# Attention of a hybrid encoder block: one pipeline of 64 units instead of four of 16, gates from high and low parts, loads moved between queues

## The reference, cut to what matters

```python
h = rmsnorm(x) * (1 + scale1) + shift1
proj = h @ w_in      # DeltaNet q,k,v,z | small | q_b,k_b,v_b (8 heads of 64) | gate_a, gate_b (1024 each)
o_a = deltanet(...)  # 4 heads of 128, both directions, chunks of 64 tokens
o_b = neighbourhood_attention(q_b, k_b, v_b, rpb)  # grid of 8 rows x 64 columns, window 8 x 16, bias per head
x = x + gate1 * ((sigmoid(gate_a) * (o_a @ w_oa) + sigmoid(gate_b) * (o_b @ w_ob)) @ w_out)
x = x + gate2 * expert_choice_moe(rmsnorm(x) * (1 + scale2) + shift2)   # 16 experts
y = rmsnorm(x) * final_g
```

## Time and profile before

| what | value |
|---|---|
| median of three runs | 2696.39 us |
| the profiled execution: its own time, its span | 2698.65 us, 2696.9 us |
| busy of the span: TensorE, VectorE, ScalarE, GpSimd | 92%, 55%, 43%, 16% |
| mean granted clock of TensorE | 0.955 |
| project, deltanet, attention, merge begin at | 86, 431, 819, 1203 us |
| route begins, experts run until | 1350, 2670 us |

### The profile page before, as it was taken

How to read it: one execution, slowest core, us unless ns; L and a number is a source line. 1 busy time by engine, 2 the same in 40 slices (tenths; PEclk the granted TensorE clock), 3 DMA queues, 4 the chain that set the end, 5 groups by cost and what they waited for, 6 DMA issues and landing times. The chain is left out here.

```text
span 2696.9 us, 39301 instructions
## 1 busy us (share of the span) xinstructions
PE 2470.2 (92%) x14796; PEld 1778.2 (66%) x14796; DVE 1488.6 (55%) x1764; ACT 1157.7 (43%) x1302; POOL 432.7 (16%) x382
## 2 busy tenths in 40 slices
PE   7799998898996999987999399999999999999994
PEld 2677886777773444443344388888888888888883
DVE  2645212555541222221211588888888888888884
ACT  2422111222212323321111377667766676777763
POOL 2101202333311000001123101111111111111101
PEclk9899998999987999998999599999999999999997
DMA  6354311000005212127221599999999999999994
GB/s 220 126 180 154 116 63 64 18 23 28 22 2 126 70 47 70 43 80 255 70 109 62 187 357 375 375 372 380 374 376 374 370 376 376 374 373 373 372 376 150
DMA packets 269040, 556.74 MB, mean 206 GB/s; under 512 B 13192, under 2 KB 66541, under 8 KB 266893
## 3 DMA queue, kind: packets, MB, share of 16 engines
q1 hardware_dynamic: 255485, 517.51, 53.4%
q0 software_dynamic: 4608, 16.78, 2.4%
q10 hardware_dynamic: 8848, 21.04, 2.2%
HBM read 511.21 MB, written 44.07 MB: 206 GB/s over the span
## 5 line engine op out<-in xcount | busy, mean ns | idle before, releaser
L2273 PE MATMUL ps<-whigh,xeT 128*128 128x512 f32 x2048 | 668.7, 400 | 9.1 <-DVE xeT L2418 9.1
L2426 DVE TENSOR_TENSOR wlow<-hT,whigh 128x2048 fp32r<-128x2048 f32 x192 | 431.9, 2284 | 84.3 <-ACT whigh L2369 84.3
L2273 PEld LDWEIGHTS ps<-whigh,xeT 128*128 128x128 f32 x2048 | 386.9, 189 | 100.1 <-issue 9.5
L2273 PE MATMUL ps<-wlow,xeT 128*128 128x512 f32 x1024 | 406.5, 397 | 0.0
L2369 ACT ACTIVATE whigh<-hT 128x2048 fp32r<-128x2048 f32 x192 | 358.5, 1910 | 17.8 <-PE ps L2273 17.8
L2273 PE MATMUL ps<-whigh,hidT 128*128 128x512 f32 x1024 | 334.6, 398 | 1.5 <-DVE hidT L2453 1.5
L2426 DVE TENSOR_TENSOR wlow<-oaT,whigh 128x2048 fp32r<-128x2048 f32 x96 | 216.7, 2285 | 50.2 <-ACT whigh L2369 50.2
L1601 PE MATMUL ps<-hT,wg 128*128 128x512 f32 x512 | 241.4, 616 | 0.0
L2426 DVE TENSOR_TENSOR wlow<-obT,whigh 128x2048 fp32r<-128x2048 f32 x96 | 217.8, 2284 | 29.6 <-ACT whigh L2369 29.6
L2273 PEld LDWEIGHTS ps<-whigh,hidT 128*128 128x128 f32 x1024 | 192.8, 188 | 47.9 <-issue 1.7
L2273 PEld LDWEIGHTS ps<-wlow,xeT 128*128 128x128 f32 x1024 | 193.5, 189 | 43.2
(11 more groups left out here) (279 smaller groups left out, 3262.7 us busy)
## 6 DMA issues: line engine op xcount, KB each, us to landing
hT<-in_w_down SPq DMA_DIRECT2D x66, 1024.0 KB, 8.5
obT<-in_w_up SPq DMA_DIRECT2D x64, 1024.0 KB, 8.6
hT<-in_w_up SPq DMA_DIRECT2D x64, 1024.0 KB, 6.2
hT<-in_w_gate SPq DMA_DIRECT2D x62, 1024.0 KB, 9.0
oaT<-in_w_down SPq DMA_DIRECT2D x62, 1024.0 KB, 6.8
oaT<-in_w_gate SPq DMA_DIRECT2D x34, 1024.0 KB, 8.8
obT<-in_w_gate SPq DMA_DIRECT2D x32, 1024.0 KB, 5.7
oaT<-in_w_ada SPq DMA_DIRECT2D x16, 1024.0 KB, 7.1
```

The costliest lines, as they stand in the source:

```text
L2273: mm = pe.matmul(out, lhs[x], rhs[y], start=start and i == 0, stop=stop and i == 2)
L2426: dve.tensor_tensor(wlow[slot][:, :], raw[(FIRST + x) % RAW_SLOTS], whigh[slot][:, :].bitcast(F32), ALU.subtract).then_inc(low_done, 1)
```

## The change

The four turns of the attention loop become one unrolled pipeline of 64 units: the outputs of pair h are turned in slots 16h+12 and 16h+20 and the v of the next pair in slots 16h+14 and 16h+22, between other work; SLOTS is 70. q and k have two buffers each, v one, and are loaded in the final order, since project's `take` now writes q, k, v in column order and scales q. The gates are computed from `hh`, `hl` (kept from project) and split gate weights, three fp32r matmuls a step, 12 a slot. `rel` is loaded, and `outside` built, at the start and at the end of deltanet's lists; several buffers move into `m["hT"]` and `m["obT"]` to make room. In merge the nine loads go from ScalarE's queue to SP's, one or more behind each turn's loads, and the weights go ahead of the gates.

```diff
@@ phase_project, take
-                        func = ACT.Silu if tile < A_TILES else ACT.Copy
-                        act.activation(out[u % 4][:, :], ps[:, u % 4, :], func).then_inc(taken, 1)
+                        if tile < A_TILES:
+                            act.activation(out[u % 4][:, :], ps[:, u % 4, :], ACT.Silu).then_inc(taken, 1)
+                        else:
+                            act.activation(out[u % 4][:, :].rearrange("p (c r) -> p r c", r=ROWS),
+                                           ps[:, u % 4, :].rearrange("p (r c) -> p r c", r=ROWS), ACT.Copy,
+                                           scale=(-DH ** -0.5 if tile < A_TILES + PAIRS else 1.0)).then_inc(taken, 1)
@@ phase_deltanet, SP (first in its list) and GpSimd (last in its list)
+                for c in range(16):
+                    src = bass.AP(a["rpb"].tensor, RPB_FRONT - 15 * c - 8, [[HB * RPB_LEN, ROWS], [RPB_LEN, HB], [1, RPB_RUN]])
+                    sp.dma_start(rel[8 * c:8 * c + 8, :, :], src).then_inc(rel_in, 16)
...
                 make_ro(NU - 1)
+                pool.memset(outside[:, :], 0.0).then_inc(outside_done, 1)
+                for step, (lo, hi, x0, x1, base, slope, cm) in enumerate((
...
+                    pool.wait_ge(outside_done, step + 1)
...
+                    pool.affine_select(out=part, in_=part, compare_op=ALU.is_ge, fill=BIG, base=base + slope * x0,
+                                       pattern=[[slope, x1 - x0], [0, 8]], channel_multiplier=cm).then_inc(outside_done, 1)
@@ phase_attention, SP
+                load_pair(0)
+                load_gate(0)
+                load_v(0)
+                load_gate(1)
+                load_pair(1)
+                for tile in range(2, GTILES):
+                    load_gate(tile)
...
@@ phase_attention, TensorE
+                def gates(count):
+                    for _ in range(count):
+                        u, r = divmod(next(products), TERMS)      # TERMS = 3 * KD
+                        k, term = divmod(r, 3)
+                        tile, g = divmod(u, GROUPS)
+                        if r == 0:
+                            pe.wait_ge(glo_done, tile + 1)
+                            if u >= 1:
+                                pe.wait_ge(gate_sb, u)
+                        w = (ghi, ghi, glo)[term][tile % 2][:, k, :]
+                        x = (hh, hl, hh)[term][:, k, g * SEQ:(g + 1) * SEQ]
+                        mm = pe.matmul(ps[:, 1, :], w, x, start=(r == 0), stop=(r == TERMS - 1))
...
+                for w in range(SLOTS):
+                    if w < NW:
+                        scores(w)
+                    if w in V_AT:
+                        turn_v(*V_AT[w])
+                    if 2 <= w < NW + 2:
+                        turn(w - 2)
+                    if w in OUT_AT:
+                        turn_out(*OUT_AT[w])
+                    if 3 <= w < NW + 3:
+                        values(w - 3)
+                    if w < NW:
+                        gates(PER_SLOT)
@@ phase_attention, ScalarE: the high part, in slots with w % 4 == 1; VectorE: the low part, w % 4 == 2
+                def split(tile):
+                    act.wait_ge(wg_in[tile % 2], 16 * (tile // 2 + 1))
+                    if tile >= 2:
+                        act.wait_ge(gate_ps, GROUPS * (tile - 1))
+                    act.activation(ghi[tile % 2][:, :, :], wg[tile % 2][:, :, :], ACT.Copy).then_inc(ghi_done, 1)
@@ phase_merge, SP
-                with sp.Fori(0, KD // 2) as jj:
+                for jj in range(KD // 2):
                     for i in range(2):
                         sp.wait_ge(wide_done, jj * (2 * JOBS) + 4 * (i + 1))
-                        sp.dma_start(graw[i]...)   # gates first, then weights
+                        sp.dma_start(wj[i][:, 0:HA, :], ...)
+                        sp.dma_start(wj[i][:, HA:KD, :], ...)
+                        sp.dma_start(graw[i][:, :, :], ...)
+                    if jj == 0:
+                        sp.dma_start(late["wout"]...)
+                    if jj == 1:
+                        sp.dma_start(late["wr"]...), (late["mul2row"]...), (norm2...), (late["gate1"]...)
+                    if jj == 2:
+                        sp.dma_start(m["hT"]..., a["x"]...)
+                    if jj == 3:
+                        sp.dma_start(late["shift2"]...), (m["gate2"]...) twice
@@ phase_merge, ScalarE
-                act.wait_ge(graw_in[0], 16)
-                ... the same nine loads, ahead of the loop of sigmoids
```

More of the change, by code:

```diff
@@ L831, in phase_deltanet @@
         ro = sb("ro", [P, TPG])
-        on = sb("on", [P, TPG, P])
+        on = first["on"]
+        rel, outside = first["rel"], first["outside"]
         tokk_ps = sem("tokk_ps")
@@ L1443, in phase_attention @@
     KIND_AT = [0, 256, 640]
-    BIAS_W = 896
+    hh, hl = m["hh"], m["hl"]
+    rel, outside = first["rel"], first["outside"]
     with ExitStack() as ctx:
@@ L1561, in _ @@
[L1561 to L1570 removed]
+                for h in range(PAIRS):
@@ new lines, in turn_v @@
+                def turn_v(h, g):
+                    if g == 0:
+                        pe.wait_ge(v_in, 16 * (h + 1))
+                    if h >= 1:
+                        pe.wait_ge(ob_done, GROUPS * (h - 1) + g + 1)
+                    if h >= 1 or g >= 1:
+                        pe.wait_ge(vtok_sb, GROUPS * h + g)
+                    for t in range(TPG):
+                        mm = pe.transpose(ps[:, 0, t * P:(t + 1) * P], vT[:, g, t * P:(t + 1) * P], ident)
+                    mm.then_inc(vt_ps, 1)
@@ new lines, in turn_out, with scores @@
+                def turn_out(h, g):
+                    pe.wait_ge(otok_done, PER_PAIR * h + (g + 1) * 2 * TPG)
+                    pe.wait_ge(vtok_sb, min(GROUPS * (h + 1) + g, GROUPS * PAIRS))
+                    if h + g:
+                        pe.wait_ge(ob_done, GROUPS * h + g)
+                    for t in range(TPG):
+                        mm = pe.transpose(ps[:, 0, t * P:(t + 1) * P], otok[:, g, t, :], ident)
+                    mm.then_inc(obT_ps, 1)
+                def scores(w):
+                    h, g, hp, t = unit(w)
+                    k0, k1 = KEY_TILES[t]
+                    if w % PER_PAIR == 0:
+                        pe.wait_ge(qk_in[h % 2], 32 * (h // 2 + 1))
+                    if w >= 2:
+                        pe.wait_ge(sc_done, w - 1)
+                    rows = slice(hp * DH, (hp + 1) * DH)
+                    pe.matmul(ps[:, 2 + w % 2, 0:width(t)], qT[h % 2][rows, g, t * P:(t + 1) * P],
+                              kT[h % 2][rows, g, k0 * P:k1 * P], start=True, stop=True).then_inc(s_ps, 1)
@@ new lines, in _ @@
+                for w in range(SLOTS):
[11 more added lines that the diff above has]
+                        gates(PER_SLOT)
+                assert not list(products)
```

420 lines of the change are left out of this document (191 added, 229 removed).

## The result

The changed kernel takes 2612.76 us (median of 4 runs, 2599.64 to 2631.30) against 2697.52 for the kernel before on the same chip (4 runs, 2696.34 to 2698.88). The ratio is 0.969, 95% interval 0.9664 to 0.9716, so it is 84.8 us faster. The forecast was 2602. The four times lie 32 us apart, where those of before lie 2.5 us apart here (20 us on another chip, 2684.16 to 2703.87), and the profiled execution is the slowest of them: 2631.30 us, span 2629.6.

What follows compares the result with a forecast made beforehand. TensorE's list was taken to bound attention (busy 348.07 of 366 us). Slots and boundaries 69.9, opening 5.85, merge 1.5 and 17.7, less 0.5 in project, make 94.5 us less, so 2602; 8-in-10 range 2589 to 2623.

Steps and rivals of the forecast that it cites:

- part 3: Attention's opening: reordering copies go, splits come; first gate product at about 832.0, not 837.85, gain 5.85; rel's loads cost nothing.
- Part 1: Attention slots: twelve fp32r matmuls replace four fp32 products; a slot takes 4.44 us, not 5.15, saving 45.4 over 64 slots.
- the prediction's own sign: Attention: gate starts wider than 0.227, or a phase longer than 315 us, would show the first part wrong.
- Part 2: Attention's three pair boundaries: one pipeline leaves only a plain slot at each; net gain 25.4 us, bounds 20 and 29.
- Part 4: Merge: first job 1.5 us earlier; without stalls the first three turns take 89.5 us, not 107.17, gain 17.7.
- rival 1: Merge: one ordered queue makes blocks wait behind w_out or x, so only its start gains; 2620 us, chance 0.06.
- Part 5: Project's end: the last take writes with a stride, 1.12 us against 0.60, adding 0.5 us.
- Rivals 2, 3 and 4: Attention: another engine's chain sets slots (2647 or 2618, 0.06); fp32r matmuls cost 0.395 (2731, 0.02); waits tie units (2625, 0.02).

Runs made afterwards that it cites:

- rel spread: Changed kernel with rel's 16 loads issued three at a time behind the loads of units 2 to 7: 2608.9 us, ratio 0.9678.
- rel wide: Changed kernel with the 16 loads carrying the same bytes over 128 partitions, from w_in: 2606.56 us, ratio 0.9675.
- shift of 32 bytes: Rel's loads spread as above, plus a 32-byte buffer ahead of the split gate weights and another ahead of the experts' split weights: 2606.71 us.
- better order: Rel's loads spread, outside built before the last ro, first gate weights loaded ahead of the first pair: 2605.87 us, ratio 0.967; 2609.16 on another chip.
- the two moves: On top of rel's spread loads: outside built before the last ro, and first gate weights loaded ahead of the first pair; 2605.87 us with both.
- the paced kernel: Changed kernel with each of rel's 16 loads issued only when the one before has landed: 2637.96 us.

## Why the prediction was right, and where it was not

**Total.** 2602 forecast, 2612.76 measured; on a second chip the same kernel took 2628.55. Without the stalls it is 2606 to 2609 in four kernels (rel spread, rel wide, shift of 32 bytes, better order). The mechanism of every gain was right; one step had a cost that I put at nothing, and one price was too low.

**The step that failed, part 3:** "`rel` is no wait any more: its 16 issues stand first in deltanet's SP list, ahead of the load of unit 2, which is wanted some 50 us later; cost nothing." The load of unit 2 was in fact in time (it landed at 489.56 us and TensorE never waited for it). What stood in no list of mine was the transfer of TensorE's own instructions. It cost 20.3 us in the profiled execution, 16.6 of them in the two long stalls; by the medians it is 3.9 us (2612.76 against 2608.9, two chips) to 22.7 (2628.55 against 2605.87 on one chip, the two moves in it). That the loads cause it is shown by taking them away, doubling them, adding them to the kernel before, and changing only their shape. That it goes by way of TensorE's instruction packets rests on their times, on the count of instructions between two of them, on stalls inside groups, and on the paced kernel; no row names the engine that a packet is for, and what delays the packets is not shown.

The Trainium skill, Runtime: NRT & Kernel Launch, section "Instruction fetch mechanics", says that each sequencer fetches its instructions over a DMA queue of its own in blocks of 16 KiB (256 instructions), "mostly hidden". The trace agrees with the block: packets of 16 KB, 4 to 5 us apart where TensorE issues 64-column products, with a median of 247 of its instructions between two. The Trainium skill, DMA: Bandwidth & Descriptors, section on why a DMA increments its semaphore by 16 and not by 1, says that a transfer gets the largest number of engines up to 16 that divides the slowest dimension of both its sides; 8 partitions would get 8. The trace agrees: a DMA share of 0.53 from 466.00 to 475.30 us, when rel's packets are nearly alone, at 63 GB/s; over 128 partitions the share was 0.81 at 290 GB/s (the loads of two units in it). Put together the two would have pointed at the rival that my list lacked.

**Part 1, slots.** 45.4 forecast, 40.3 measured. The count of products and the rest of a slot (1.72 us) were right; the term that was mis-sized is the spacing, 0.2267 taken from project where attention has 0.2340: 768 x 0.0073 = 5.6 us. By the prediction's own sign (gate starts wider than 0.227) this price was wrong. My bound said that no row had one cheaper than 0.227; I had not looked for dearer ones, though the experts' rows of the kernel before show them (0.234).

**Part 2, boundaries.** 25.4 forecast, 23.6 measured, within 20 to 29. **Part 3's opening** itself: 5.85 against 6.3. First gates came 9.46 us behind the first issue (9.9 forecast), and the 2.8 us of selects are there (2.76). **Part 4:** 19.2 forecast, 18.9 in the changed kernel and 20.3 alone. Turns of 29.20 us; the queue's margins held, so rival 1 (one ordered queue) did not come. The first job was 1.2 us slower than the row of before (9.99 against 8.79); its mean granted clock was 0.69 against 0.79. **Part 5:** 0.5 forecast; the last take went from 0.60 to 1.08 us, and deltanet's start is 1.6 later, 1.1 of which no step of mine explains (the other profiles with this project phase have it 0.3 to 1.8 later). Rivals 2, 3 and 4 are out: from 900 to 1100 us TensorE was busy in all of the 200 us, a product cost 0.234 and not its length of 0.395, and between the first gate product and the end of attention TensorE's longest idle time was 0.5 us.

**The range** holds the measured total, but for the wrong reason: its upper end was set by rivals that did not happen, and a loss that was not listed moved the total towards it. That is luck: the same kernel's 2628.55 on the second chip lies outside 2589 to 2623.

## What to carry to other kernels

A load that "nothing waits for" can still hold up the transfers that bring instructions. Before placing a batch of loads of few partitions, ask how long it will drain (bytes over the rate of a like row, here 2.9 MB at 63 GB/s, 46 us) and which engine runs dense, short instructions meanwhile; spread the batch behind later units, or give it 128 partitions. And take a product's price from all rows of its kind, the dear ones too: two streams of the same instruction differ by 3% here, and moving a buffer by 416 bytes took that away in the experts, 30 us (one run).

## What the hardware showed that was not expected

- Sixteen loads of 180 KB over 8 partitions drain at 60 to 70 GB/s with a DMA share of about a half; a cqkv load of 768 KB issued behind them took 37.0 us to land, against 5.2. One at a time they take 5.3 us each.
- Under that backlog TensorE's instruction packets, from the second of the stage to the fourth, come 8 to 17 us apart, where the kernels with no such loads at that place have 4 to 5, and TensorE stops in the middle of a group for 6.4 to 9.4 us where the gap was 13 us or more.
- fp32r products of 512 columns at full clock start 0.227 us apart in project and 0.234 in the experts. Moving xeT and hidT (and the buffers around them) by 416 bytes turned the one into the other in the experts (one run); moving weights and data together by 32 bytes did not. In the attention, moving the weights by 32 or 416 bytes gave 0.2324 and 0.2297 in place of 0.2340. The combination of the 416 bytes with the better order was not run.
